# An expert loop whose first block is taken out of the loop and put ahead of the block list

## The reference, cut to what matters

```python
logits = jnp.dot(xf, w_router) + b_router
vals, idx = lax.top_k(logits, TOP_K)          # TOP_K = 4
gate = jax.nn.softmax(vals, axis=-1)
...
def expert_block(args):
    xb, eb = args
    up = jnp.dot(xb, w_up[eb]) + b_up[eb]
    glu, lin = jnp.split(up, 2, axis=-1)
    glu = jnp.minimum(glu, SWIGLU_LIMIT)
    lin = jnp.clip(lin, -SWIGLU_LIMIT, SWIGLU_LIMIT)
    act = glu * jax.nn.sigmoid(SWIGLU_ALPHA * glu) * (lin + 1.0)
    return jnp.dot(act, w_down[eb]) + b_down[eb]
...
out = jnp.zeros((N + 1, D_)).at[row_tok].add(yb * row_gate[:, None])
```

## Time and the profile before

| | |
|---|---|
| Median of 3 runs | 2135.1 us (2130.39 to 2138.82) |
| Profiled execution, its own time | 2135.09 us |
| Its span in the trace | 2133.2 us |
| TensorE (PE) busy | 1996.2 us, 94% |
| DVE, ScalarE (ACT) busy | 473.1 us, 315.1 us |
| Read from HBM | 550.41 MB |

### The profile page before, as it was taken

The page is one execution under the profiler, slowest core; times in us unless marked ns, Lnnn a source line. Parts: engine busy times, 40 slices in busy tenths (PEclk is TensorE's granted clock), DMA queues, the critical chain, the costliest instruction groups (busy, mean ns, idle before and its releaser), DMA issues.

```text
span 2133.2 us, 25748 instructions
## 1 busy us (share of the span) xinstructions
PE 1996.2 (94%) x10136; PEld 1207.5 (57%) x10137; DVE 473.1 (22%) x1205; ACT 315.1 (15%) x682; POOL 3.7 (0%) x14
## 2 busy tenths in 40 slices
PE   7998778999999999999999998998999999899999
PEld 5786464333333333333333333777788878688887
DVE  2212632111111111111111112463101024521100
ACT  1111401111111111111111111151000003400000
POOL 0000000000000000000000000000000000000000
PEclk9998686999999999999999999998999999999999
DMA  9867022999999899999998999732344552334340
GB/s 309 260 217 276 1 87 113 417 417 418 419 416 395 356 417 418 418 419 418 417 417 342 417 417 382 226 112 68 116 127 109 150 179 76 119 118 146 102 108 20
DMA packets 247692, 552.34 MB, mean 259 GB/s; under 512 B 18552, under 2 KB 181090, under 8 KB 214738
## 3 DMA queue, kind: packets, MB, share of 16 engines
q1 hardware_dynamic: 236336, 547.96, 68.0%
q10 hardware_dynamic: 11298, 3.54, 0.8%
HBM read 550.41 MB, written 1.06 MB: 259 GB/s over the span
## 4 chain that ended last, share of the span: by engine, by line
PE 65%; DMA 11%; SPq 8%; DVE 4%; issue 2%; ACT 1%; ACTq 0%; POOL 0%; DVEq 0%
PE bank L1600 18%; PE bank L1344 12%; DMA ring<-in_w_up_dram 11%; SPq L1292 7%; PE bank L1366 7%; PE bank L1813 7%; PE bank L1605 4%; PE bank L1323 2%; PE bank L1305 2%; PE bank L1704 2%; PE bank L1708 2%; PE bank L1210 1%; PE bank L1336 1%; DVE act_t_e L1449 1%; PE bank L1580 1%
## 5 line engine op out<-in xcount | busy, mean ns | idle before, releaser
L1344 PE MATMUL bank<-ring,x_expert 128*64 128x512 f32 x2176 | 489.3, 598 | 30.9 <-DMA ring<-in_w_up_dram 30.7
L1600 PE MATMUL bank<-hT,ring 128*128 128x272 f32 (+1 forms) x1664 | 377.0, 390 | 12.4 <-DVE hT L2030 6.3
L1600 PEld LDWEIGHTS bank<-hT,ring 128*128 128x128 f32 x1664 | 319.0, 192 | 70.4 <-issue 14.0
L1344 PEld LDWEIGHTS bank<-ring,x_expert 128*64 128x64 f32 x2176 | 147.7, 137 | 371.0 <-issue 278.9
L1366 PE MATMUL bank<-ring,act_t_e 128*64 128x512 f32 x1088 | 241.0, 595 | 6.9 <-DVE act_t_e L1449 6.9
L1366 PEld LDWEIGHTS bank<-ring,act_t_e 128*64 128x64 f32 x1088 | 77.6, 137 | 148.3 <-issue 148.3
L1813 PE MATMUL bank<-ffn_act,ring 128*128 128x272 f32 (+1 forms) x704 | 158.1, 386 | 0.0
L1813 PEld LDWEIGHTS bank<-ffn_act,ring 128*128 128x128 f32 x704 | 133.7, 190 | 22.8
L1441 DVE TENSOR_SCALAR glu<-bank 128x512 f32<-128x512 f32 x34 | 23.5, 692 | 439.2 <-PE bank L1344 439.2
L1396 ACT ACTIVATE sig<-glu 128x512 f32<-128x512 f32 x34 | 21.4, 630 | 534.8 <-DVE lin L1442 534.8
L1605 PE MATMUL bank<-ring,hT 128*128 128x256 f32 x384 | 85.5, 381 | 0.0
(11 more groups left out here) (444 smaller groups left out, 1543.9 us busy)
## 6 DMA issues: line engine op xcount, KB each, us to landing
ring<-in_w_up_dram SPq DMA_DIRECT2D x256, 1024.0 KB, 19.1
ring<-in_w_down_dram SPq DMA_DIRECT2D x128, 1024.0 KB, 21.5
ring<-in_w_gu_dram SPq DMA_DIRECT2D x44, 1024.0 KB, 5.2
ring<-in_w_in_dram SPq DMA_DIRECT2D x33, 1024.0 KB, 8.4
ring<-in_w_ada_dram SPq DMA_DIRECT2D x24, 1024.0 KB, 10.1
ring<-in_w_down_dram SPq DMA_DIRECT2D x32, 704.0 KB, 6.6
ring<-in_w_out_dram SPq DMA_DIRECT2D x12, 1024.0 KB, 8.1
cst<-in_consts_dram SPq DMA_DIRECT2D x1, 1361.5 KB, 9.9
```

The lines of the kernel that those rows point to most:

```text
L1344: ins = mm(bank[CAP * half:CAP * half + CAP, :], xe[:, k, :], ring[:, k, a:a + 512], start=False, stop=(k == CHUNKS - 1))
L1600: ins = mm(bank[:, 0:columns], w[:, k, P * m:P * m + P], src[:, k, 0:columns], start=(k == 0), stop=(k == CHUNKS - 1))
```

## The change

The first block (expert 0) is written out ahead of the loop, and it no longer waits for the table. The loop of TensorE begins with block 1; the loops of DVE and ScalarE still begin with 0, but their preparation for block 0 moves up into the router's part.

- DVE: after `picked`, the one-hot of expert 0, then the places and the selector of block 0 straight after `placed`; then the other places and the block list (`listed`); then the gates, `lam_in` and `gains`; then the table; the decay and lambda results last, behind the table (`lam_read`). The two memsets of `ye` and `pgt` go.
- ScalarE: the copy of the gathered rows and that of their turned columns stand behind the logarithm of the decay work and ahead of the copy of the gates.
- TensorE: gather and turning of block 0, then the turning of the list, the up biases and products of block 0, with the turning of the gates and the lambda product in their middle (`turn_gates`); the gather of block 1; the 8 down-bias products in place of block 0's scatter; then block 0's down products, and the loop.
- SP's program is unchanged.

The core of the diff:

```diff
@@ -619,6 +621,11 @@
             act.activation(lam_sum[:, 1:2], lam_sum[:, 0:1], ACT.Exp).then_inc(s["lam_exp"], 1)
             st(act.activation(lru_c[:, 1, :], lru_c[:, 0, :], ACT.Exp))
             act.activation(lru_c[:, 2, :], lru_c[:, 1, :], ACT.Ln, bias=ones[:, 0:1]).then_inc(s["lru_log"], 1)
+            act.wait_ge(q1["gathered"], 1)
+            act.activation(xrow[:], pb[3][:], ACT.Copy).then_inc(q1["x_copied"], 1)
+            act.wait_ge(q1["x_turned"], 1)
+            act.activation(xe[:].rearrange("p (h c) n -> p c h n", h=2), pb[0][:].rearrange("p (c h n) -> p c h n", c=4, h=2), ACT.Copy)\
+               .then_inc(q1["x_rows"], 1)
             act.wait_ge(s["gates_turned"], 1)
             act.activation(gtT[:], pb[5][0:E, 0:S], ACT.Copy).then_inc(s["gates_t"], 1)
...
@@ -867,6 +874,33 @@
             picked = RW[:, 5, :, :]
             st(tt(picked, RW[:, 2, :, :], RW[:, 0, :, :], ALU.add))
             dve.sem_inc(s["logits_ready"], 1)
+            dve.sem_inc(expert_used, EXPERT_SLABS)
+            dve.memset(pmx[:, :, E1 - 1:E1], -1.0)
+            dve.tensor_copy(hot[:], C["twice"][0:2 * E, 0:1].broadcast_to([2 * E, CAP])).then_inc(q1["hot_ready"], 1)
+            for name in ("y_rows", "pg_rows", "u_free", "pg_turned"):
+                dve.sem_inc(q1[name], 1)
+            dve.wait_ge(s["placed"], 1)
+            places = pb[7][:, 0:2 * E].rearrange("p (t e) -> p t e", t=TT)
+            st(stt(pmx[:, :, 0:E], places, 1.0, picked, ALU.add, ALU.mult))
+            st(ts(pmx[:, :, 0:E], pmx[:, :, 0:E], -1.0, None, ALU.add))
+            for t in range(TT):
+                ins = ts(psel[:, t, :], C["iota"][:, 0:CAP], pmx[:, t, 0:1], None, ALU.is_equal)
+            ins.then_inc(q1["sel_ready"], 1)
+            for b in range(1, BLOCKS):
+                ts(pmx[:, :, E * b:E * b + E], pmx[:, :, 0:E], -float(CAP * b), None, ALU.add)
+
+            by_expert = over[:, 0, :].rearrange("p (e b) -> p e b", b=BLOCKS)
+            st(dve.tensor_copy(over[:, 5, 0:E], pb[7][:, 2 * E:3 * E]))
+            dve.memset(by_expert[:, :, 0], 1.0)
+            for b in range(1, BLOCKS):
+                ins = ts(by_expert[:, :, b], over[:, 5, 0:E], float(CAP * b), None, ALU.is_gt)
+            st(ins)
+            st(dve.tensor_tensor_scan(over[:, 1, :], ones[:, 0:OVER], over[:, 0, :], 0.0, ALU.mult, ALU.add))
+
+            st(stt(over[:, 2, :], over[:, 1, :], C["number"][:, 0:1], over[:, 0, :], ALU.is_equal, ALU.mult))
+            st(tt(over[:, 3, :], over[:, 2, :], C["column"][:, 0:OVER], ALU.mult))
+            dve.tensor_reduce(pickc[:], over[:, 3, :], AX_X, ALU.add).then_inc(s["listed"], 1)
+
             dve.wait_ge(s["logit_exp"], 1)
             st(tt(RW[:, 4, :, :], RW[:, 4, :, :], picked, ALU.mult))
             st(dve.tensor_reduce(RS[:, 1, :], RW[:, 4, :, :], AX_X, ALU.add))
...
@@ -874,8 +908,7 @@
             st(tt(gx[:, :, 0:E], RW[:, 4, :, :], spread_last(RS[:, 2, :], E), ALU.mult))
             for b in range(1, BLOCKS):
                 dve.tensor_copy(gx[:, :, E * b:E * b + E], gx[:, :, 0:E])
-            dve.memset(gx[:, :, E1 - 1:E1], 0.0)
-            dve.memset(pmx[:, :, E1 - 1:E1], -1.0).then_inc(s["gates_ready"], 1)
+            dve.memset(gx[:, :, E1 - 1:E1], 0.0).then_inc(s["gates_ready"], 1)
             lru = PC[:, r2["lru_L_2"]:r2["lru_L_2"] + 8]
             st(tt(LQ[:], LQ[:], LK[:], ALU.mult))
...
@@ -885,32 +918,6 @@
                 a = r2["subln_g_2"] + l
                 ts(gains[:, l:l + 1], PC[:, a:a + 1], 1.0 - LAM_INIT[l], None, ALU.mult)
-            dve.wait_ge(s["placed"], 1)
-            places = pb[7][:, 0:2 * E].rearrange("p (t e) -> p t e", t=TT)
-            st(stt(pmx[:, :, 0:E], places, 1.0, picked, ALU.add, ALU.mult))
-            st(ts(pmx[:, :, 0:E], pmx[:, :, 0:E], -1.0, None, ALU.add))
-            for b in range(1, BLOCKS):
-                ins = ts(pmx[:, :, E * b:E * b + E], pmx[:, :, 0:E], -float(CAP * b), None, ALU.add)
-            dve.wait_ge(s["lru_log"], 1)
-            st(stt(lru_c[:, 0, :], lru, 0.0, lru_c[:, 2, :], ALU.min, ALU.subtract))
-            ts(lru_c[:, 1, :], lru_c[:, 0, :], LRU_C, None, ALU.mult)
-            ts(lru_c[:, 2, :], lru_c[:, 0, :], -LRU_C, None, ALU.mult)
-
-            dve.wait_ge(s["lam_made"], 1)
-            for l in range(L2):
-                ts(lam[:, l:l + 1], pb[4][:, l:l + 1], -1.0, -LAM_INIT[l], ALU.mult, ALU.add)
-
-            by_expert = over[:, 0, :].rearrange("p (e b) -> p e b", b=BLOCKS)
-            st(dve.tensor_copy(over[:, 5, 0:E], pb[7][:, 2 * E:3 * E]))
-            dve.memset(by_expert[:, :, 0], 1.0)
-            for b in range(1, BLOCKS):
-                ins = ts(by_expert[:, :, b], over[:, 5, 0:E], float(CAP * b), None, ALU.is_gt)
-            st(ins)
-            st(dve.tensor_tensor_scan(over[:, 1, :], ones[:, 0:OVER], over[:, 0, :], 0.0, ALU.mult, ALU.add))
-
-            st(stt(over[:, 2, :], over[:, 1, :], C["number"][:, 0:1], over[:, 0, :], ALU.is_equal, ALU.mult))
-            st(tt(over[:, 3, :], over[:, 2, :], C["column"][:, 0:OVER], ALU.mult))
-            dve.tensor_reduce(pickc[:], over[:, 3, :], AX_X, ALU.add).then_inc(s["listed"], 1)
             dve.wait_ge(s["list_turned"], 1)
             items = lists[0:1, 0, :]
             st(dve.tensor_copy(items, pb[6][0:1, 256:256 + ITEMS + 1]))
...
@@ -919,11 +926,20 @@
                 st(ts(lists[0:1, 2, :], items, float(E * b), -float(E), ALU.is_ge, ALU.mult))
                 st(tt(lists[0:1, 1, :], lists[0:1, 1, :], lists[0:1, 2, :], ALU.add))
             st(tt(lists[0:1, 3, :], items, lists[0:1, 1, :], ALU.add))
-            dve.sem_inc(expert_used, EXPERT_SLABS)
             done_by = over[0:1, 1, :].rearrange("p (e b) -> p e b", b=BLOCKS)[:, :, BLOCKS - 1]
             dve.tensor_copy(table[0:1, 0, :], items)
             dve.tensor_copy(table[0:1, 1, :], lists[0:1, 3, :])
             dve.tensor_copy(table[0:1, 2, 0:E], done_by).then_inc(s["table_ready"], 1)
+
+            dve.wait_ge(s["lru_log"], 1)
+            st(stt(lru_c[:, 0, :], lru, 0.0, lru_c[:, 2, :], ALU.min, ALU.subtract))
+            ts(lru_c[:, 1, :], lru_c[:, 0, :], LRU_C, None, ALU.mult)
+            ts(lru_c[:, 2, :], lru_c[:, 0, :], -LRU_C, None, ALU.mult)
+
+            dve.wait_ge(s["lam_made"], 1)
+            for l in range(L2):
+                ins = ts(lam[:, l:l + 1], pb[4][:, l:l + 1], -1.0, -LAM_INIT[l], ALU.mult, ALU.add)
+            ins.then_inc(s["lam_read"], 1)
         def tensor_block1(pe):
...
@@ -1324,9 +1326,7 @@
                                  start=False, stop=False, skip_group_check=True)
                 ins.then_inc(done, 1)
-            gather(0)
-            turn_rows(0)
-            with pe.Fori(0, count) as i:
+            def up(i, e, halfway=None):
                 pe.wait_ge(q["hot_ready"], i + 1)
                 pe.wait_ge(q["u_free"], i + 1)
                 pe.wait_ge(q["x_rows"], i + 1)
...
@@ -1335,17 +1335,17 @@
                         r = slice(E * b, E * b + E)
                         ins = mm(bank[CAP * half:CAP * half + CAP, :], hot[r, :], bup[r, 512 * half:512 * half + 512], start=True, stop=False)
                 ins.then_inc(q["bias_used"], 1)
-                e = pass_expert(pe, i)
                 for k in range(CHUNKS):
+                    if halfway and k == CHUNKS // 2:
+                        halfway()
                     pe.wait_ge(*arrived(k, e))
                     for b, bank in enumerate((bankU0, bankU1)):
                         for half in range(2):
                             a = D * b + 512 * half
                             ins = mm(bank[CAP * half:CAP * half + CAP, :], xe[:, k, :], ring[:, k, a:a + 512], start=False, stop=(k == CHUNKS - 1))
                     ins.then_inc(expert_used, 1)
-                pe.wait_ge(q["pg_rows"], i + 1)
-                gather(i + 1)
-                scatter(i, q["scattered"])
+
+            def down(i, e):
                 pe.wait_ge(q["act_ready"], i + 1)
                 for c in range(4):
                     ins = tp(bankY[:, P * c:P * c + P], act_e[:, P * c:P * c + P], ident)
...
@@ -1366,18 +1366,44 @@
                         ins = mm(bankY[CAP * half:CAP * half + CAP, :], rows_, w[:, 512 * half:512 * half + 512], start=(k == 0), stop=(k == CHUNKS - 1))
                     if k % 2:
                         ins.then_inc(expert_used, 1)
+
+            gather(0)
+            turn_rows(0)
+            pe.wait_ge(s["listed"], 1)
+            tp(pb[6][0:1, 256:256 + ITEMS + 1], pickc[0:ITEMS + 1, :], ident[0:ITEMS + 1, 0:ITEMS + 1]).then_inc(s["list_turned"], 1)
+            pe.wait_ge(s["biases_in"], 48)
+
+            def turn_gates():
+                pe.wait_ge(s["gates_ready"], 1)
+                for t in range(TT):
+                    ins = tp(pb[5][0:E, P * t:P * t + P], gx[:, t, 0:E], ident)
+                ins.then_inc(s["gates_turned"], 1)
+                pe.wait_ge(s["lam_exp"], 1)
```

(54 more changed lines are left out.)

26 lines of the change are left out of this document (2 added, 24 removed).

## The result

The changed kernel takes 2125.5 us (median of 10 runs, 2117.21 to 2129.27) against 2134.6 us for the kernel before (10 runs, 2130.39 to 2141.24). The ratio is 0.9946, interval 0.9934 to 0.9958: 9.1 us or 0.54% faster (0.42 to 0.66%), where 12.3 us were forecast.

The account below looks back on a forecast made before the run. The prediction took the start of the experts' weight stream to bound the kernel. Head start 13.6 us less 1.3 us given back in block 0 is 12.3 us, so 2135.1 - 12.3 = 2122.8 us, range 2117.5 to 2130 us.

Parts of the forecast that it names:

- The bound: Expert stage: time follows the start of the weight stream; a start N us earlier moves everything behind by N.
- The head start, 13.6 us: SP's first slab issue of the loop comes at 343.5 us instead of 357.13.
- What block 0 gives back, 1.3 us: Block 0: first down slab released 21.4 us behind the first up slab, beyond 20.1, so the stream idles 1.3 us.
- the second sign of being wrong: Lead shrinking by more than 2 us between SP's first issue and its first restart.
- rival 2: Clock at 2.4 GHz from the router's products on, or rising with the first bias products; 2119.5 us, chance 0.12.
- The sum: Whole kernel: net gain of 12.3 us, from 2135.1 to 2122.8 us.
- the forecast's own part: Whole kernel: the forecast's own range, 2119.5 to 2125.5 us, chance 0.55.
- rival 1: Block 0 slower: later clock rise, late DVE selector or stall at loop entry; costs 2 to 6 us, chance 0.2.
- Rivals 3 and 4: Head start goes nowhere, 2130 to 2135 us, chance 0.08; clock at 1.2 GHz through block 0, about 2146 us, 0.05.

Follow-up runs that it names:

- the repeat: The changed kernel, unedited, traced in a second execution; 2130.3 us (1 run).
- table_first: Changed kernel with the list turned first and block 0's gather waiting for the table again; 2126.6 us, ratio 0.9961.
- bias_padded: Changed kernel with weights and gates of the down-bias products padded with zeros from 32 to 128 rows; 2124.2 us (1 run).
- filled: Changed kernel with ScalarE's row copies first and block 0's down biases divided, two behind the gather, two behind each of three down slabs; 2119.6 us.

## Why the prediction was right, and where not

**The bound.** Right, and the base of the rest: the expert stage hangs on the start of the stream, and its two restarts carry a shift to the end. The first DMA wait of an up product was forecast at 515 us and came at 522.20: at expert 2 the stream was only 2.0 us behind its releases (369.96 + 4 x 2.51 against 378.01), where before it was 2.9 us behind (357.13 + 30.1 against 384.35), so TensorE took longer to catch up with it. The restarts don't show a cost of that.

**The head start, 13.6 us.** 12.8 in the profiled execution, 14.1 in the repeat, both counted from the picked experts. By the bare times of the two profiles it was 10.8 us. The prediction had called itself wrong outside 13 to 14 us, and neither execution lies inside: the first misses it by 0.2 us even when counted from the picked experts, the repeat by 0.1 to the other side. The path was the one foretold: the copy of the gathered rows stood right behind the logarithm at 338.02 us, 2.1 us behind the end of the gather. The difference between the two executions is the clock under the five count products, 0.61 us a pair instead of 0.39. The three ScalarE operations with the table load took 1.8 us to the start of the copy (336.20 to 338.02), so no drain behind the load showed: the load itself took 1.28 us, and the logarithm started 0.01 us behind its end. The page ScalarE: Activation LUTs of the Trainium skill, section What ACT_TABLE_LOAD costs, has 2.66 us for the switch. This trace doesn't agree.

**What block 0 gives back, 1.3 us.** This is the term that was mis-sized: it measured 3.5 us in the profile and 4.8 in the repeat. It is also the second sign of being wrong that the prediction had named: the lead shrank by 3.6 us up to the first restart, and not by less than 2. The step said that the down biases take 3.6 us at full clock, kept the clock's rise 3.9 us behind the first up product, and left the clock at 1.00 from there on. The products do take that (3.7 us in table_first and padded). But in the profile the rise came 5.1 us behind the first up product, which costs 0.6 us, and behind the biases the clock fell in four of five executions, so that the turns and the first down products ran at half pace, which costs 1.7 us in the profile and 3.4 in the repeat. Where the clock stayed, the hole was 1.4 us (table_first) and 1.6 us (bias_padded): the 1.3 us were right for the work and wrong for the clock. In the kernel before the same products ran at 0.50 anyway, so no row of it could show the fall; that they didn't raise the clock in 7 us was there to be read, and I used it only against rival 2.

**The sum.** 12.3 foretold, 9.1 by the medians; 12.8 - 3.5 = 9.3 in the profile and 14.1 - 4.8 = 9.3 in the repeat. The number lies inside the stated range, but at 2125.5 us it is the last value of the forecast's own part of it, and inside rival 1's. That it was faster at all is clear; that it was so by more than 0.5% isn't, with 0.54% and an interval from 0.42 to 0.66%.

**The rivals.** Rival 1 happened in its size (2125 to 2129 us). Of its three causes the later rise of the clock had a part, 0.6 us; the fall behind the biases, the larger part, it didn't name. The selector wasn't late, and the loop's entry cost nothing: TensorE goes from the last down product into the loop's first bias products without a gap.

```profile
367.64 7.29 PE L1366 MATMUL bank<-ring,act_t_e 128*64 128x512 f32 x32
374.86 1.09 PE L1336 MATMUL bank<-b_up_sb,hot 32*64 32x512 f32 x8
```

The Trainium skill, Runtime: NRT & Kernel Launch, section Instruction fetch mechanics, says that a taken branch out of the pages already fetched waits for a DMA. No wait of that kind shows at this entry. Rival 2 (full clock from the router on) didn't show in the changed kernel, but did in three traces with ScalarE's copies first. Rivals 3 and 4 fell: the restarts moved with the stream, and in the traces in which the clock was low at their start, the up products raised it within 5.2 us.

What stays open: why table_first alone kept its clock with unpadded products, and how often the changed kernel does in its timed runs; only two of its executions have a trace.

## What to carry to other kernels

In a stage that hangs on a stream, price an early start at the first release, then walk the stream slab by slab through the first pass: each release later than its slab time is a hole, and a hole takes back the head start one for one. Put work that is moved off a serial stretch where the stream has slack, in small pieces between releases, and under a wait that is there anyway; filled had a hole of 0.3 us that way. Don't carry a clock read in the old place over to the new one: ask what the moved work itself does to it.

## What the runs showed of the hardware

TensorE at 100% busy fell to half clock behind a run of 32-row products: 13.7 us at 0.50 for 32 of them, none with the same products padded to 128 rows (11.27 against 7.17 us, one execution each); for 16 of them in four of five executions, and in none of two padded ones. At full clock, a wait of 4.4 us ahead of block 0's turning went with a fall in six of six executions, and one of 0.7 us with none in three. SP needed 1.66 us from the finished table to its first issue that depended on it (333.43 to 335.09, and 338.95 to 340.61).
